# Joining the expert scatter by a plain selection, and reordering the opening's small loads and the store of x

## The reference

```python
def expert_choice_ffn(h, w_router, b_router, w_gate, w_up, w_down):
    B, S, D = h.shape
    cap = (EC_CAPACITY_FACTOR * S) // N_EXPERTS              # 64
    logits = (h @ w_router + b_router).astype(jnp.float32)
    affinity = jax.nn.softmax(logits, axis=-1)
    gates, idx = lax.top_k(affinity.transpose(0, 2, 1), cap)
    bidx = jnp.arange(B)[:, None, None]
    xin = h[bidx, idx]
    hid = jax.nn.silu(jnp.einsum('becd,edf->becf', xin, w_gate)) * jnp.einsum('becd,edf->becf', xin, w_up)
    y = jnp.einsum('becf,efd->becd', hid, w_down) * gates[..., None].astype(h.dtype)
    return jnp.zeros_like(h).at[bidx, idx].add(y)
```

## Time and profile before

| | |
|---|---|
| median of 3 runs | 3030.18 us (3027.91 to 3034.47) |
| the profiled execution's own time | 3035.36 us |
| its span (first to last instruction) | 3033.3 us |
| PE busy, share of the span | 2778.2 us, 92% |
| DVE, ACT, POOL busy | 954.8, 678.1, 201.6 us |
| expert loop | about 547 to 1524 us of the span |

### The profile page before, as it was taken

How to read it: one execution, slowest core, us unless ns; L and a number is a source line. 1 busy time by engine, 2 the same in 40 slices (tenths; PEclk the granted TensorE clock), 3 DMA queues, 4 the chain that set the end, 5 groups by cost and what they waited for, 6 DMA issues and landing times.

```text
span 3033.3 us, 36505 instructions
## 1 busy us (share of the span) xinstructions
PE 2778.2 (92%) x15636; PEld 1939.5 (64%) x15636; DVE 954.8 (31%) x1550; ACT 678.1 (22%) x1153; POOL 201.6 (7%) x149
## 2 busy tenths in 40 slices
PE   6989676999999999999989988999999988999998
PEld 3756455533444344434477848999999784788886
DVE  4555544011111111111153253433224334433323
ACT  3214432100010001000132142322223224222222
POOL 2303010000000000000020310000000050000000
PEclk8989887899999999999989969999999996999998
DMA  7262013799999999999911101223332110132321
GB/s 254 90 243 78 1 30 148 308 403 421 418 414 406 417 416 414 405 417 415 349 42 56 49 14 56 84 72 103 89 86 58 56 63 1 56 103 85 111 76 57
DMA packets 238575, 558.33 MB, mean 184 GB/s; under 512 B 29601, under 2 KB 191779, under 8 KB 213500
## 3 DMA queue, kind: packets, MB, share of 16 engines
q1 hardware_dynamic: 234160, 548.48, 47.5%
q0 software_dynamic: 1552, 5.70, 0.6%
q10 hardware_dynamic: 2748, 2.47, 0.3%
HBM read 552.39 MB, written 4.23 MB: 184 GB/s over the span
## 4 chain that ended last, share of the span: by engine, by line
PE 85%; DVE 8%; ACT 3%; issue 2%; DMA 1%; SPq 1%; ACTq 0%; DVEq 0%; POOL 0%; PEldq 0%; POOLq 0%
PE vpsum L2109 19%; PE vpsum L1979 15%; PE apsum L2109 11%; PE vpsum L1996 7%; PE apsum L1963 4%; PE apsum L2118 3%; PE vpsum L2021 2%; PE apsum L2021 2%; PE apsum L2135 2%; PE vpsum L2135 2%; PE vpsum L1761 2%; PE vpsum L1752 1%; PE vpsum L2250 1%; PE vpsum L1837 1%; PE apsum L2039 1%
## 5 line engine op out<-in xcount | busy, mean ns | idle before, releaser
L1979 PE MATMUL vpsum<-ring,arena 128*64 128x512 f32 x2048 | 448.8, 596 | 0.8 <-ACT arena L959 0.8
L2109 PE MATMUL vpsum<-work_r,wring_r 128*128 128x264 f32 (+1 forms) x2160 | 347.7, 323 | 3.4 <-DVE work_r L1613 3.4
L2109 PEld LDWEIGHTS vpsum<-work_r,wring_r 128*128 128x128 f32 x2160 | 313.4, 190 | 37.9 <-issue 6.0
L2109 PE MATMUL apsum<-stream_r,wring_r 128*128 128x264 f32 (+1 forms) x2208 | 336.1, 312 | 0.0
L1979 PEld LDWEIGHTS vpsum<-ring,arena 128*64 128x64 f32 x2048 | 144.8, 137 | 290.9 <-issue 290.9
L2109 PEld LDWEIGHTS apsum<-stream_r,wring_r 128*128 128x128 f32 x2208 | 308.2, 192 | 22.2 <-issue 1.2
L1517 DVE TENSOR_TENSOR wring_r<-wring,wring_r 128x2048 fp32r<-128x2048 f32 (+2 forms) x97 | 200.2, 2069 | 348.3 <-ACT wring_r L1009 348.3
L2109 PE MATMUL vpsum<-stream_r,wring_r 128*128 128x264 f32 (+1 forms) x1728 | 273.8, 318 | 10.5 <-DVE body L1600 10.5
L1009 ACT ACTIVATE wring_r<-wring 128x2048 fp32r<-128x2048 f32 (+3 forms) x100 | 172.6, 1728 | 466.6 <-DMA wring<-w_ffn 450.3
L2109 PEld LDWEIGHTS vpsum<-stream_r,wring_r 128*128 128x128 f32 x1728 | 247.1, 192 | 31.8 <-DVE body L1600 10.9
L1996 PE MATMUL vpsum<-ring,arena 128*64 128x512 f32 x1024 | 226.8, 595 | 11.0 <-ACT arena L971 11.0
(11 more groups left out here) (424 smaller groups left out, 3120.6 us busy)
## 6 DMA issues: line engine op xcount, KB each, us to landing
ring<-w_gate SPq DMA_DIRECT2D x64, 2048.0 KB, 16.6
ring<-w_up SPq DMA_DIRECT2D x64, 2048.0 KB, 9.6
ring<-w_down SPq DMA_DIRECT2D x64, 2048.0 KB, 13.0
wring<-w_ffn SPq DMA_DIRECT2D x88, 512.0 KB, 4.7
ring<-w_ada SPq DMA_DIRECT2D x12, 2048.0 KB, 13.8
wring<-w_ffn SPq DMA_DIRECT2D x32, 704.0 KB, 4.5
ring<-w_in SPq DMA_DIRECT2D x5, 2048.0 KB, 12.5
wring<-w_in SPq DMA_DIRECT2D x10, 1024.0 KB, 5.5
```

What stands on the lines that cost most here:

```text
L1979: last = pe.matmul(banks[g][CAP * blk:CAP * blk + CAP, :], xin[:, 2 * r + c, :], w[:, at:at + 512], start=r + c == 0, stop=r + c == 4)
L2109: last = pe.matmul(dst, w_[:, c, col:col + P], x_.bitcast(FR), start=c == 0 and i == 0, stop=c == chunks - 1 and i == 2)
```

## The change

In the expert loop, PE transposes `sel` instead of `selg`, and ACT copies it out as fp32r (`selT_r`; zeros and ones). Four more f32 matmuls of one column, `selg` transposed times a column of ones, give the gate of each slot; ACT copies this column to `slot_gate`. When y is ready, ACT writes its high part times the gate (`ye_hi`, fp32r, `scale=slot_gate`), DVE writes the rest (`ye_lo` = y * gate - `ye_hi`), and PE scatters with two fp32r matmuls per 128 features in place of one f32 matmul. The first four pairs wait for the low part of the first half (`ye_low`), the last four also for that of the second half; the waits on `acc_done` stay.

In the opening, ACT issues the 30 small DMAs first, then splits `in0`, then issues the store of x.

```diff
--- before.py
+++ after.py
@@ -112,6 +112,9 @@
         with ExitStack() as names:
             ring_r = names.enter_context(nc.sbuf_tensor("ring_r", [P, NSLOT, SLOT], F32))
             first_r = names.enter_context(nc.sbuf_tensor("first_r", [P, KC * S], F32))
+        with ExitStack() as names:
+            names.enter_context(nc.sbuf_tensor("ring_room", [P, NSLOT, SLOT], F32))
+            arena_r = names.enter_context(nc.sbuf_tensor("arena_r", [P, ARENA], F32))
         with ExitStack() as names:
             wring = names.enter_context(nc.sbuf_tensor("wring", [P, NSLOT2, SLOT2], F32))
             body = names.enter_context(nc.sbuf_tensor("body", [P, BODY], F32))
@@ -320,12 +323,13 @@
         top8 = arena[0:NE, M0 + 2048:M0 + 2056]
         sel = region(M0 + 2560, TT * 2 * CAP, "p (t a c) -> p t a c", t=TT, a=2)
         selg = region(M0 + 3072, TT * 2 * CAP, "p (t a c) -> p t a c", t=TT, a=2)
-        selT = region(M0 + 3584, S, "p (a t) -> p a t", a=1)
+        selT_r = arena_r[:, M0 + 3584:M0 + 3584 + S]
         xin = region(M0 + 4096, KC * CAP, "p (c n) -> p c n", c=KC)
         sg = region(M0 + 4608, 2 * 512, "p (g f) -> p g f", g=2)
         hid = region(M0 + 5632, 2 * 512, "p (g f) -> p g f", g=2)
         hidT = region(M0 + 6656, 2 * 512, "p (g j n) -> p g j n", g=2, j=4)
-        ysb = region(M0 + 7680, D, "p (a d) -> p a d", a=1)
+        ye_hi, ye_lo = arena_r[:, M0 + 7680:M0 + 7680 + D], arena_r[:, M0 + 4608:M0 + 4608 + D]
+        slot_gate = sb("slot_gate", [P, 1])
         slots_iota = region(M0 + 8704, TT * 2 * CAP, "p (t a c) -> p t a c", t=TT, a=2)
         assert M0 + 9216 <= ARENA
 
@@ -351,7 +355,8 @@
         hT_copied = sem("hT_copied")
         xin_copied = sem("xin_copied")
         selT_copied = sem("selT_copied")
-        y_copied = sem("y_copied")
+        ye_high, ye_low = sem("ye_high"), sem("ye_low")
+        gate_summed, gate_copied = sem("gate_summed"), sem("gate_copied")
         hid_done = sem("hid_done")
         sel_done = sem("sel_done")
         acc_done = sem("acc_done")
@@ -800,8 +805,6 @@
                     act.wait_ge(*HIGH_FREE[i])
                 act.activation(ring_r[:, HIGH_SLOT[i], :].bitcast(FR), ring[:, at, :], ACT.Copy).then_inc(in_high, 1)
 
-            act.dma_start(x_d, arena[:, R3:R3 + 4096]).then_inc(x_stored, 16)
-            input_high(Q_W)
             vec(rowsA, ROW_N2, a["norm2_g"][0], 8)
             for w in range(TAPS):
                 vec(rowsA, ROW_CW + 4 * w, a["conv_w"][0, w], 4)
@@ -823,6 +826,8 @@
                     vec(rowsB, o, a[nm][l], n)
                     o += n
             act.dma_start(btab, a["const_buckets"]).then_inc(bias_in, 16)
+            input_high(Q_W)
+            act.dma_start(x_d, arena[:, R3:R3 + 4096]).then_inc(x_stored, 16)
             for c in range(KC):
                 act.wait_ge(h_done, c + 1)
                 act.activation(f_hi[:, c, :].bitcast(FR), hT[:, c, :], ACT.Copy).then_inc(h_high, 1)
@@ -965,14 +970,17 @@
                     act.activation(sg[:, g, :], G_BANK[g][:, :], ACT.Silu).then_inc(silu_done, 1)
                     if g == 0:
                         act.wait_ge(selT_done, e + 1)
-                        act.activation(selT[:, 0, :], SELT_BANK[:, :], ACT.Copy).then_inc(selT_copied, 1)
+                        act.activation(selT_r.bitcast(FR), SELT_BANK[:, :], ACT.Copy).then_inc(selT_copied, 1)
+                        act.wait_ge(gate_summed, e + 1)
+                        act.activation(slot_gate[:], XIN_BANK[:, 0:1], ACT.Copy).then_inc(gate_copied, 1)
                 for g in range(2):
                     act.wait_ge(hT_done, 2 * e + g + 1)
                     act.activation(arena[:, M0 + 6656 + 512 * g:M0 + 7168 + 512 * g], HT_BANK[g][:, :], ACT.Copy).then_inc(hT_copied, 1)
                 copy_tokens(e + 2)
                 act.wait_ge(down_done, 2 * e + 2)
                 for i in range(2):
-                    act.activation(ysb[:, 0, 512 * i:512 * i + 512], Y_BANK[i][:, :], ACT.Copy).then_inc(y_copied, 1)
+                    act.wait_ge(gate_copied, e + 1)
+                    act.activation(ye_hi[:, 512 * i:512 * i + 512].bitcast(FR), Y_BANK[i][:, :], ACT.Copy, scale=slot_gate[:, 0:1]).then_inc(ye_high, 1)
 
             def warm_root(n):
 
@@ -1450,6 +1458,10 @@
                     if g == 0:
                         dve.wait_ge(selT_done, e + 1)
                         select(e + 2, e + 1)
+                for i in range(2):
+                    dve.wait_ge(ye_high, 2 * e + i + 1)
+                    dve.scalar_tensor_tensor(ye_lo[:, 512 * i:512 * i + 512].bitcast(FR), Y_BANK[i][:, :], slot_gate[:, 0:1], ye_hi[:, 512 * i:512 * i + 512],
+                                             ALU.mult, ALU.subtract).then_inc(ye_low, 1)
                 for c in range(KC):
                     dve.wait_ge(scatter_done, 8 * e + c + 1)
                     dve.tensor_tensor(acc[:, c, :], acc[:, c, :], OUT_BANK[c % 4][:, :], ALU.add).then_inc(acc_done, 1)
@@ -2003,8 +2015,11 @@
                 up(e, 0, G_BANK)
                 pe.wait_ge(sel_done, 2 * e + 2)
                 for t in range(TT):
-                    last = pe.transpose(SELT_BANK[:, t * P:t * P + P], selg[:, t, :, :].rearrange("p a c -> p (a c)"), ident[:])
+                    last = pe.transpose(SELT_BANK[:, t * P:t * P + P], sel[:, t, :, :].rearrange("p a c -> p (a c)"), ident[:])
                 last.then_inc(selT_done, 1)
+                for t in range(TT):
+                    last = pe.matmul(XIN_BANK[:, 0:1], selg[:, t, :, :].rearrange("p a c -> p (a c)"), ones[:, 0:1], start=t == 0, stop=t == TT - 1)
+                last.then_inc(gate_summed, 1)
                 pe.wait_ge(acc_done, 8 * e + 1)
                 up(e, 4, U_BANK)
                 transpose_hidden(e, 0)
@@ -2013,12 +2028,15 @@
                 gather(e + 2)
                 down(e, 1)
 
-                pe.wait_ge(y_copied, 2 * e + 2)
                 pe.wait_ge(selT_copied, e + 1)
                 for c in range(KC):
+                    if c % 4 == 0:
+                        pe.wait_ge(ye_low, 2 * e + 1 + c // 4)
                     if c >= 4:
                         pe.wait_ge(acc_done, 8 * e + c - 2)
-                    pe.matmul(OUT_BANK[c % 4][:, :], ysb[:, 0, c * P:c * P + P], selT[:, 0, :], start=True, stop=True).then_inc(scatter_done, 1)
+                    for y, last_part in ((ye_hi, False), (ye_lo, True)):
+                        last = pe.matmul(OUT_BANK[c % 4][:, :], y[:, c * P:c * P + P].bitcast(FR), selT_r.bitcast(FR), start=not last_part, stop=last_part)
+                    last.then_inc(scatter_done, 1)
 
             pe.wait_ge(acc_done, 8 * NE + 1)
             pe.wait_ge(xin_copied, NE + 1)
```

## The result

The changed kernel takes 2999.35 us (median), the kernel before beside it 3030.75; the ratio is 0.989, with a 95% interval of 0.987 to 0.991. A second series gave 2997.89 against 3032.45 (0.989, 0.987 to 0.990). Forecast were 2997 us and a move of -33.3; the two series moved by -31.4 and -34.6. One run of the changed kernel (3633 us) and the only run of the experiment pool_late_loop_end had a lower TensorE clock all through, and their times are not used.

What follows compares the result with a forecast made beforehand. PE's own chain was taken to set the loop's pace, DMA close behind, and loads the opening's. Loop 28.5 + sixteenth 0 + opening 4.8 = 33.3 us off 3030.18 gave 2997 us, range 2990 to 3004 (8 in 10: 2987 to 3009).

Steps and rivals of the forecast that it cites:

- The pass: Expert loop: one pass falls from 60.88 to 59.0 us, minus 1.9 net; fifteen passes give 28.5 us.
- The stretch: Loop scatter, from ACT's first copy of y to the next pass's first matmul: from 8.20 to 5.5 us.
- that rival is out: Loop scatter: DVE's adds, 0.86 us apart even without waiting, set the pace; time 3009 us; chance 0.06.
- Gate matmuls: Between the halves of `up` on PE: four added one-column f32 matmuls cost 0.79 us a pass.
- The weights' floor: Loop weight loads: 25.17 MB a pass at 429 GB/s take 58.7 us, so a pass cannot be shorter.
- That rival did not come true: Loop weight loads: weights bound the loop, at 422 GB/s a pass takes 59.6 us; time 3006 us; chance 0.15.
- the slower rival: Loop: PE's clock falls after waits of 1.6 us instead of 1.2, and the change loses time; chance 0.03.
- The sixteenth gives nothing: Last scatter, behind the loop: the path waits for POOL's three subtractions, so the shorter scatter gains 0 us.
- a slipped-in L1510: Loop's end: one more DVE instruction between POOL's subtractions about pays for the last 0.79 us of gate matmuls.
- The opening: Before the loop: the later store of x lets `in0` land at 39.0 instead of 43.8 us, giving 4.8 us.
- the small loads' issue gives nothing: Opening: hiding 6.4 us of small-load issue ahead of the high parts of h brings no time back.
- DVE held by GpSimd: Opening and loop's end: a DVE instruction reading two SBUF operands stands still while POOL subtracts; opposite rival in the opening 0.05.

Runs made afterwards that it cites:

- pool_late_loop_end: Changed kernel, GpSimd's three subtractions behind the loop held until DVE's last sum part, four pieces each; only run had a low TensorE clock, time not used.
- no_gate, experiment 5: Changed kernel without the four gate matmuls, y scattered without its gate; 2985.84 us.
- experiment 6, no_gate_high_only: Changed kernel without gate matmuls and without y's low part, eight scatter matmuls that do not wait for DVE; 2992.31 us.
- experiment 8: Changed kernel, GpSimd's three subtractions behind the loop held until DVE's last sum part, four pieces each; 2991.42 us in repeated runs.
- opening_only, experiment 1: Kernel before with only the opening's new order (small loads, split of `in0`, store of x); 3026.34 us, ratio 0.9988.
- scatter_only, experiment 2: Changed kernel with the old opening, so only the new scatter; 3002.72 us, ratio 0.9909.
- experiment 4, vecs_only: Kernel before with the 30 small loads first, then the store of x, then the split of `in0`; 3025.91 us, one run.
- store_only, experiment 3: Kernel before with the store of x moved behind the split of `in0`, the 30 small loads still behind both; 3024.16 us, one run.
- the pieces, experiment 7: Changed kernel with GpSimd's first subtraction in the opening cut into eight pieces of 512 columns; 2996.43 us once, 2997.54 us in repeated runs.
- experiment 9: The changed kernel unchanged, timed again beside its GpSimd variants in the same series; 2997.89 us.
- both_pool, experiment 10: Changed kernel with GpSimd's first subtraction in eight pieces and its three behind the loop held and cut; 2985.18 us, ratio to before 0.985.
- late_again: Changed kernel, GpSimd's three subtractions behind the loop held until DVE's last sum part, four pieces each, timed in repeated runs; 2991.42 us.

## Why the prediction was right, point by point

- **The pass** was forecast at 59.0 us and is 59.02. The stretch: 5.5 forecast, 5.56 measured; PE's wait for DVE 1.6, measured 1.67; sixteen matmuls and the small loss to the adds 3.9 (907.76 to about 911.7), measured 3.94; adds 0.60 us apart behind each other (from 898.29 to 899.48, two of them), so they don't set the pace, and that rival is out. Gate matmuls: 0.79 by the row, 0.79 a pass in no_gate, 0.88 in their own row.
- **The weights' floor** of 58.7 us was right: 58.73 by the beat of the waits in experiments 5 and 6. That rival did not come true, at 0.3 us from where it begins. "HBM Reference" (Trainium skill, section "Specifications (TRN2)") gives about 425 GB/s for a core alone; by that a pass would have been an estimated 59.2 us. The loop moved 426 GB/s with PE setting the pace and 428 where the weights did, so the figure is close. "DMA: Bandwidth & Descriptors" (Trainium skill, section "Where 436 GB/s comes from") has the HBM side bind at about 358 GB/s. The measured 413 to 428 GB/s of every loop here contradict that for this core.
- **The clock in the loop** stayed at 1.00 through waits of 1.67 us, so the slower rival is out. Its mechanism is real in the same loop: experiments 5 and 6 have slower matmuls at a lower clock behind waits of 0.87 to 2.32 us, though not behind each. That a wait of 1.67 us left no trace is therefore no general allowance.
- **"The sixteenth gives nothing"** was the term that was off in size: it costs about 1 us. The forecast counted 15 x 1.9 = 28.5 us. From the loop's first load to the projection the lead grows by 30.99 - 4.15 = 26.84. The split: 14 passes between the rows of the table give 26.03 (1.86 each, not 1.9), the first stretch loses 0.77 (gate matmuls with no scatter ahead of them), the stretch up to the last scatter gains 1.87 (ACT's copies start at 1514.98 before, at 1483.70 after), and behind that 0.29 is lost, to ACT's copies with a pointer (1.26 us where two plain ones took 1.08), which let GpSimd start 0.19 later, and to 0.1 from there on. Sixteen groups of gate matmuls stand against fifteen shorter scatters that count. I had let a slipped-in L1510 pay for the sixteenth group; it can't, since the path leaves from GpSimd's end: 17.82 us from there to the projection before (1532.00 to 1549.82), 17.90 after (1500.93 to 1518.83). That the cover hid the shorter scatter was right: held back, GpSimd's work gave the 2.6 us and more (experiment 8).
- **The opening**: 4.8 forecast, 4.68 at `in0`'s landing, 4.15 at the loop's first load in the changed kernel and 4.57 in opening_only. In time it is 3.6 us by the ratio of opening_only (0.9 to 6.7), and 3.4 or 4.8 between scatter_only and the two medians of the full change (2999.35, 2997.89). That the small loads' issue gives nothing was right, and store_only shows it. What I had not seen is that moving them alone would have done (experiment 4): I had let a store issued before `in0` lands take its bytes from `in0` in any case, but its packets start 3.7 us or more behind the issue.
- **DVE held by GpSimd** was argued from two rows and is now shown: by three starts with nearly one end (experiments 1 and 3) and by the pieces (7, 8). "SBUF — State Buffer" (Trainium skill, section "🔬 SBUF: two separate sides") states this rule: the port pair that the two engines share is an exclusive lock for a whole instruction, taken by whichever starts first, and a DVE instruction with two SBUF inputs needs it against a GpSimd instruction that reads SBUF. The trace agrees: 8.90 us for 0.68. L1245, with one SBUF input, was held as well, 1.48 us between GpSimd's pieces and 0.53 behind them. The section also counts a DVE instruction in a 2-port mode among those that need the pair; whether L1245 ran in such a mode no run here shows.
- **Luck**: there was some in the profiled executions. Their move of 34.6 us is 4.15 in the opening (0.65 less than forecast), 26.84 in the loop (1.7 less) and 3.6 in the second block, which the forecast had at nothing. These 3.6 most likely belong to the one profiled execution of before: it took 5.2 us more than that kernel's median, and its second block 1483.5 us, where the same code took 1479.7 to 1480.7 in opening_only, store_only and vecs_only. The medians of the first series hold no such gift: 4.15 + 26.84 = 31.0, and they moved by 31.4. Those of the second series moved by 34.6, within the interval of the first; its traces hold no second one of before that could divide the difference.

**What stays open**: what decides the clock that PE is granted in the second block. The table under experiment 9 shows that the block's length follows it, from 1473 us (both kernels that hold GpSimd back) over about 1480 (most) to 1484 and 1487 (the pieces in the opening alone). The two traces of the changed kernel agree within 0.4 us and those with the pieces within 2, so it looks tied to the program; yet no_gate has 1475.0 without holding GpSimd back, the four runs of both_pool spread over 8 us, and most kernels have one trace. So 7 of the 13 us that both_pool's profiled execution gained, and some 4 of the 6.5 us of late_again, can't be promised to another kernel.

## What to carry to other kernels

Ask of a stretch that gets shorter what else must end before the path goes on: fifteen scatters paid, the sixteenth lay under GpSimd's subtractions while its added work stood in the open. A GpSimd instruction of 4 to 9 us beside DVE work with two SBUF inputs that the path needs held that work until its end here; cut it, or start it behind. In a loop where weights come within 0.3 us of binding, further savings on the engine end there: no_gate's 0.79 us a pass gave 0.48, and no_gate_high_only's further 1.1 us gave nothing. A store issued beside awaited loads took their place only 3.7 us and more behind its issue (experiment 4), so late in the wait it cost nothing. A total that is off by less than some 7 us should be split at fixed events before a cause is named.
